# Two half-sized products of the down projection moved from the fourth-last block slot to the end, and the last product's two output tiles finished one by one

## What is computed

```python
def rmsnorm(x, g):
    xf = x.astype(jnp.float32)
    y = xf * lax.rsqrt(jnp.mean(xf * xf, axis=-1, keepdims=True) + EPS)
    return (y * g.astype(jnp.float32)).astype(x.dtype)

def swiglu(x, w_gate, w_up, w_down):
    return (jax.nn.silu(x @ w_gate) * (x @ w_up)) @ w_down
...
        xp = xp + swiglu(rmsnorm(xp, norm2_g[l]), w_gate[l], w_up[l], w_down[l])
...
    y_prompt = rmsnorm(xp, final_g)
```

## Time and profile before

| | |
|---|---|
| median of 3 executions | 2186.22 us (2185.85 to 2186.42) |
| the profiled execution | 2186.3 us |
| its span, first to last instruction | 2184.6 us |
| PE, matmuls: busy | 2170.5 us (99%) |
| VectorE: busy | 1714.3 us (78%) |
| ScalarE: busy | 1003.8 us (46%) |
| mean granted TensorE clock | 0.999 |
| moved by DMA | 325.63 MB, mean 149 GB/s |

### The profile page before, as it was taken

How to read it: one execution, slowest core, us unless ns; L and a number is a source line. 1 busy time by engine, 2 the same in 40 slices (tenths; PEclk the granted TensorE clock), 3 DMA queues, 4 the chain that set the end, 5 groups by cost and what they waited for, 6 DMA issues and landing times.

```text
span 2184.6 us, 40850 instructions
## 1 busy us (share of the span) xinstructions
PE 2170.5 (99%) x17316; PEld 2164.5 (99%) x17316; DVE 1714.3 (78%) x1988; ACT 1003.8 (46%) x1331; POOL 12.6 (1%) x16
## 2 busy tenths in 40 slices
PE   9999999999999999999999999999999999999997
PEld 9999999999999999999999999999999999999997
DVE  7765478446796789888887888888888888787888
ACT  7433523124354455444444544444444545444455
POOL 0000000000000000000000000000000000000001
PEclk9999999999999999999999999999999999999999
DMA  5332324245333434345445445444545876555523
GB/s 191 95 109 88 107 69 145 79 144 189 117 107 99 155 108 169 128 144 165 141 134 165 142 132 155 154 131 141 165 145 164 302 287 216 193 199 199 188 78 121
DMA packets 121584, 325.63 MB, mean 149 GB/s; under 512 B 10703, under 2 KB 51215, under 8 KB 120433
## 3 DMA queue, kind: packets, MB, share of 16 engines
q1 hardware_dynamic: 120928, 323.82, 44.1%
q10 hardware_dynamic: 528, 0.07, 0.0%
HBM read 267.22 MB, written 56.63 MB: 148 GB/s over the span
## 4 chain that ended last, share of the span: by engine, by line
PE 98%; DVE 1%; ACT 0%; issue 0%; POOL 0%; POOLq 0%; DVEq 0%; ACTq 0%
PE acc L1617 24%; PE acc L1302 21%; PE g L1617 18%; PE acc L1625 12%; PE g L1625 9%; PE acc L1526 2%; PE acc L1564 2%; PE g L1526 2%; PE g L1564 2%; PE g L1518 1%; PE acc L1518 1%; PE g L1329 0%; PE g L1452 0%; PE g L1321 0%; PE g L1459 0%; PE g L1351 0%
## 5 line engine op out<-in xcount | busy, mean ns | idle before, releaser
L1123 ACT CAST w_hi<-w_s 128x1024 fp32r<-128x1024 f32 (+1 forms) x204 | 209.1, 1025 | 356.0 <-DVE w_s L2414 349.8
L1617 PE MATMUL g<-op_hi,w_hi 128*128 128x272 f32 x1056 | 272.2, 288 | 0.0
L1617 PE MATMUL acc<-op_hi,w_hi 128*128 128x272 f32 x1056 | 271.6, 288 | 0.4 <-ACT acc L1097 0.4
L1617 PE MATMUL g<-op_lo,w_hi 128*128 128x272 f32 x1056 | 271.9, 288 | 0.0
L1617 PE MATMUL acc<-sg_hi,w_hi 128*128 128x272 f32 x1056 | 271.8, 288 | 0.0
L1617 PE MATMUL acc<-op_lo,w_hi 128*128 128x272 f32 x1056 | 271.4, 288 | 0.0
L1617 PE MATMUL acc<-sg_lo,w_hi 128*128 128x272 f32 x1056 | 271.4, 288 | 0.0
L1302 PE MATMUL acc<-op_hi,w_hi 128*128 128x272 f32 x1280 | 267.6, 290 | 0.0
L1302 PE MATMUL acc<-op_hi,w_lo 128*128 128x272 f32 x1280 | 264.8, 288 | 0.0
L1302 PE MATMUL acc<-op_lo,w_hi 128*128 128x272 f32 x1280 | 264.7, 288 | 0.0
L2389 DVE TENSOR_TENSOR w_lo<-w_s,w_hi 128x1024 fp32r<-128x1024 f32 (+1 forms) x204 | 242.7, 1190 | 11.8 <-ACT w_hi L1123 5.9
(11 more groups left out here) (390 smaller groups left out, 4672.7 us busy)
## 6 DMA issues: line engine op xcount, KB each, us to landing
w<-w_gu SPq DMA_DIRECT2D x88, 512.0 KB, 3.3
w_raw<-w_gu SPq DMA_DIRECT2D x88, 512.0 KB, 4.1
w_raw<-w_in SPq DMA_DIRECT2D x64, 512.0 KB, 3.6
hf_dram<-hf_hi SPq DMA_DIRECT2D x22, 952.0 KB, 6.5
hf_dram<-hf_lo SPq DMA_DIRECT2D x22, 952.0 KB, 8.8
w_raw<-w_d SPq DMA_DIRECT2D x32, 512.0 KB, 4.3
w<-w_d SPq DMA_DIRECT2D x26, 512.0 KB, 3.3
op_hi<-hf_dram SPq DMA_DIRECT2D x16, 544.0 KB, 7.1
```

The source lines that it names most:

```text
L1123: nc.scalar.copy(w_hi[:, (C_ST + n) % RING, 0:w], src[:, 0:w]).then_inc(hi_ready, 1)
L1617: nc.tensor.matmul(out, w_h, x, start=fresh and j == 0 and i == 0, stop=False, skip_group_check=True)
```

## The change

In slot 63 (`HELD`) only products 0, 1, 2, 5 and 4 run, in that order. Its products 3 and 6, which only concern the first half of the tokens, are computed at the end: the last slot runs nine, `0, 1, 2, 5, 4, 3, 3, 6, 6`, where the seventh and the ninth are slot 63's. For them SyncE loads blocks 3 and 2 of slot 63's weights again, into the two halves of `w_raw`, once the last slot's `sum_block` 2 has read these. The ring numbering shifts by two behind slot 63 (`at`).

Slot 63 then has no copy `pb` to `pd`: its C22 step adds `pb` to both token halves in one instruction of twice the width, once product 4 is done, and its C21 step is empty. C11 only needs product 0, and waits for `seeded`.

At the end, the row sums of the second half are computed between the two sides of the seventh product. The ninth product signals `side_done` after its first side; each of its two output tiles is added, squared, scaled with the gain and summed by PE on its own (`last_output`, `last_square`, `last_gain`). The squares of C11's part are added by VectorE instead of PE. The stores of the second half leave from other places of `y_second`, since product 3 still reads one that was used before.

```diff
+HELD = TAIL - 1
+HELD_ORDER = (0, 1, 2, 5, 4)
+LAST_ORDER = HELD_ORDER + (3, 3, 6, 6)
...
+            sp.wait_ge(s_made, 4 * NS - 1)
+            for i, j in enumerate((3, 2)):
+                sp.dma_start(w_raw[:, i, :], w_d4[4 * (HELD - FT - 2 * BATCHES) + j]).then_inc(held_in[i], 16)
...
             for s in range(1, NS - 1):
-                for idx in range(NP):
+                for idx in range(NP if s != HELD else len(HELD_ORDER)):
+                    if s == HELD and idx >= 3:
+                        bank_copy(s, idx + 1)
+                        block_hi(s, idx, copied=True)
+                        if idx == 4:
+                            bank_copy(s, 6)
+                        continue
...
             part_square(0)
+            act.wait_ge(chunk_done, done(at(NS - 1) + 3))
+            block_hi(NS - 1, 7, copied=True)
             part_square(1)
             act.wait_ge(c_read, 4 * NS + 4 + 2)
             seed_d(NS - 1)
+            act.wait_ge(chunk_done, done(at(NS - 1) + 4))
+            block_hi(NS - 1, 8, copied=True)
             part_gain(0)
             part_gain(1)
             row_std(1, pc[:, 1, 0:TH], 2)
             copy_factor(1, pc[:, 0, 0:TH], 1)
             part_square(2)
-            part_square(3)
             part_gain(2)
+            for q in range(2):
+                last_square(q)
+                last_gain(q)
             row_std(0, pa[:, 0, 0:TH], 3)
-            part_gain(3)
             copy_factor(0, pa[:, 1, 0:TH], 2)
...
+            product(C_ST + n + 6, n + 6, (0,), h, e_held, which=3, ends=False)
+            pe.wait_ge(c_read, read + 1)
+            pe.wait_ge(part_add, 1)
+            square_sums(pc[:, 1, 0:TH], (rstd[:, TH:T],))
+            product(C_ST + n + 6, n + 6, (1,), h, e_held, which=3)
+            down_wait(NS - 1, 6)
+            product(C_ST + n + 7, n + 7, (0, 1), h, e, which=6)
+            product(C_ST + n + 8, n + 8, (0,), h, e_held, which=6, ends=False).then_inc(side_done, 1)
+            product(C_ST + n + 8, n + 8, (1,), h, e_held, which=6)
             pe.wait_ge(c_read, read + 3)
-            pe.wait_ge(part_sq, 3)
-            square_sums(pa[:, 0, 0:TH], (rstd[:, 0:TH], sq4[2][:, 0, :], sq4[2][:, 1, :]), stop=False)
-            pe.wait_ge(part_sq, 4)
-            square_sums(pa[:, 0, 0:TH], (sq4[3][:, 0, :], sq4[3][:, 1, :]), start=False)
+            pe.wait_ge(part_add, 2)
+            square_sums(pa[:, 0, 0:TH], (rstd[:, 0:TH],), stop=False)
+            for q in range(2):
+                pe.wait_ge(part_sq, 4 + q)
+                square_sums(pa[:, 0, 0:TH], (sq4[3][:, q, :],), start=False, stop=q == 1)
...
-                dve.wait_ge(chunk_done, done(n + ((5, 4, 3, 6) if s == NS - 1 else (3, 4, 5, 6))[piece]))
+                dve.wait_ge(chunk_done, done(n + ((6, 4, 3, 8) if s == NS - 1 else (0, 4, 3, 4) if s == HELD else (3, 4, 5, 6))[piece]))
...
+                elif piece == C22 and s == HELD:
+                    nc.vector.tensor_tensor(y[:, :, 1, :, :], y[:, :, 1, :, :],
+                                            pb[:, :, 0:TH].unsqueeze(2).to_broadcast([P, 2, 2, TH]), ALU.add)\
+                        .then_inc(c_read, 1)
+                elif piece == C21 and s == HELD:
+                    dve.nop().then_inc(c_read, 1)
...
+            def last_output(q):
+                if q == 0:
+                    dve.wait_ge(side_done, 1)
+                else:
+                    dve.wait_ge(chunk_done, done(at(NS - 1) + 8))
+                y = rows(BATCHES - 1)[:, q, 1, 0, :]
+                nc.vector.tensor_tensor(y, y, pd[:, q, 0:TH], ALU.add).then_inc(c_read, 1)
+                dve.wait_ge(c_read, 4 * NS + 8 + q)
+                dve.nop().then_inc(y_part, 1)
...
             outputs(last, C22)
+            block_lo(last, 6)
             dve.wait_ge(hsq_add, 2 * KT - 2)
             add_part(0)
             add_part(1)
             dve.nop().then_inc(part_add, 1)
-            block_lo(last, 6)
+            block_lo(last, 7)
             row_factor(1, 1)
             outputs(last, C11)
             scale(1, pc[:, 0, 0:TH], (0,))
-            outputs(last, C21)
-            scale(1, pc[:, 0, 0:TH], (2, 4, 6))
+            block_lo(last, 8)
+            add_part(2)
+            dve.nop().then_inc(part_add, 1)
+            scale(1, pc[:, 0, 0:TH], (2,))
+            last_output(0)
+            scale(1, pc[:, 0, 0:TH], (4,))
+            last_output(1)
+            scale(1, pc[:, 0, 0:TH], (6, 8))
             row_factor(0, 2)
-            scale(1, pc[:, 0, 0:TH], (8,))
             scale(0, pa[:, 1, 0:TH], range(0, NV_OUT, 2))
```

More of the change, by code:

```diff
@@ L269, in build @@
         kv = trunk[:, 4:KT, :].rearrange("p (s m) t -> p s m t", s=NQ)
-        y_out = [[y[:, f, 0:HP, :] for f in range(4)] for y in (y_first, y_second)]
+        y_out = [[y[:, f, i:i + HP, :] for f, i in places]
+                 for y, places in ((y_first, ((0, 0), (1, 0), (2, 0), (3, 0))), (y_second, ((0, 0), (2, 0), (3, 0), (0, HP))))]
         aside = hid.rearrange("p (q r) t -> p q r t", q=2)
@@ L469, in product_at, with held_block @@
         def product_at(s, pos):
-            return LAST_ORDER[pos] if s == NS - 1 else pos
+            return LAST_ORDER[pos] if s == NS - 1 else HELD_ORDER[pos] if s == HELD else pos
+        def held_block(s, pos):
+            return s == NS - 1 and pos in (6, 8)
         def columns(s):
@@ L1087, in bank_copy @@
             def bank_copy(s, idx):
-                act.wait_ge(chunk_done, done(NP * s + idx - 4))
-                if idx == 1 and s >= 2:
+                act.wait_ge(chunk_done, done(at(s) + idx - 4))
+                if idx == 1 and s >= 2 and s - 1 != HELD:
                     seed_d(s - 1)
@@ L1114, in block_hi @@
                 which = product_at(s, idx)
-                if which in (0, 3):
+                src = block_of(s, which)
+                if held_block(s, idx):
+                    i = (6, 8).index(idx)
+                    act.wait_ge(held_in[i], 16)
+                    src = w_raw[:, i, :]
+                elif which in (0, 3):
                     act.wait_ge(blk_in[which], 16 * (s + 1))
@@ L1627, in product @@
                     last.then_inc(chunk_done, 1)
+                return last
             def quad(c, n, s, first=False, second=False):
@@ L1683, in _, with down_wait @@
                     quad(i * (4 * NP) + (C_ST + NP * q), NP * q, i * 4 + q)
+            def down_wait(s, idx):
+                if idx == 0:
+                    pe.wait_ge(c_read, 4 * s + C11 + 5)
+                elif idx == 1:
+                    pe.wait_ge(c_read, 4 * s + C12 + 5)
+                elif idx == 2:
+                    pe.wait_ge(seeded, s + 1)
+                elif idx == 4:
+                    pe.wait_ge(u2_out, s + 1)
+                elif idx == 5:
+                    pe.wait_ge(p5_out, s + 1)
+                elif idx == 6:
+                    pe.wait_ge(seeded_d, seeds_d(s))
             for s in range(FT, NS - 1):
                 ch, b = divmod(s - FT, BATCHES)
[L1686 to L1698, removed]
+                for pos, idx in enumerate(HELD_ORDER if s == HELD else range(NP)):
+                    down_wait(s, idx)
                     if b == 0:
                         pe.wait_ge(form_in[idx], 32 * (ch + 1))
-                    product(C_ST + NP * s + idx, NP * s + idx, (0, 1), PAIRS_H[ch], 4 * (ch % 2))
+                    product(C_ST + at(s) + pos, at(s) + pos, (0, 1), PAIRS_H[ch], 4 * (ch % 2), which=idx)
             def square_sums(out, bufs, start=True, stop=True):
@@ L1708, in square_sums @@
                     last.then_inc(var_done, 1)
[L1710 to L1728, removed]
@@ L1729, in _ @@
-            pe.wait_ge(c_read, read + 3)
-            pe.wait_ge(part_sq, 3)
-            square_sums(pa[:, 0, 0:TH], (rstd[:, 0:TH], sq4[2][:, 0, :], sq4[2][:, 1, :]), stop=False)
-            pe.wait_ge(part_sq, 4)
-            square_sums(pa[:, 0, 0:TH], (sq4[3][:, 0, :], sq4[3][:, 1, :]), start=False)
+            n, read = at(NS - 1), 4 * NS + 4
+            h, e, e_held = PAIRS_H[NCH - 1], 4 * ((NCH - 1) % 2), 4 * ((NCH - 2) % 2)
+            for pos, idx in enumerate(HELD_ORDER + (3,)):
+                down_wait(NS - 1, idx)
+                product(C_ST + n + pos, n + pos, (0, 1), h, e, which=idx)
@@ L2629, in _ @@
                         sum_block(s, 2)
+                    if s == HELD and idx == 2:
+                        sum_block(s, 3)
                     if idx == 2 and FT < s <= TAIL:
                         summands(s - 1)
-                    if idx == 3:
+                    if idx == 3 and s != HELD:
                         sum_block(s, 3)
```

42 lines of the change are left out of this document (28 added, 14 removed).

## The result

The changed kernel takes **2189.32 us** (median of 20, 2189.07 to 2190.16) against 2186.02 us before (median of 20): a ratio of 1.0015, 95% interval 1.0008 to 1.0022. That is 3.3 us more, inside the 0.2% that I had named as the bound of "no change", and just inside the range (2184.2 to 2189.4), but 2.5 us above the forecast of 2186.8.

A forecast was written before the change was run, and what follows sets the result against it. The prediction took PE's matmul stream and what follows it as the bound. Stall +2.86, tail -1.76 and stores -0.5 summed to +0.6 us, giving 2186.8 us, with an 8-in-10 range of 2184.2 to 2189.4.

The forecast's parts named there:

- The frame and slot 63: Around slot 63: 3.00 us a product, 21.02 a slot, PE's total unchanged, no wait there or for slot 64's loads.
- The stall in slot 64: Slot 64: C22 of slot 63 waits for product 4, delaying VectorE's queue and the seeded copy; PE stalls 2.86 us.
- The tail: End of the last slot: second root at 2171.38 against 2173.14 in the frame before, a win of 1.76 us.
- Rival 3: Last slot: VectorE late, low part 8's 0.4 us cover gone or side adds behind scales, +0.5 to 2 us; chance 0.13.
- Rival 4: Tail isn't shortened because the DMA engines bind anyway: +2.9 us, 2189.1; chance 0.05.
- Rival 1: Slot 64: PE isn't held for the copy, only the tail's win is left: 2183.9 us; chance 0.12.
- The stores: Behind the second root: the first half's first store finds DMA engines free, winning 0 to 0.7 us, taken as 0.5.
- Rival 2: Slot 64: PE's holes drop the granted clock; one product at 1.2 GHz gives 2189.8, two 2192.8 us; chance 0.05.

The follow-up runs named there:

- the run with the copy first: Changed kernel with ScalarE's copy pa to pb in slot 64 placed ahead of the casts of products 2 and 3: 2189.03 us.
- GpSimd later alone: Changed kernel with GpSimd starting to scale the second half's tiles only after VectorE has added the squares of C11's part: 2186.91 us.
- the run with both repairs: Changed kernel with C22 of slot 63 added after product 1's low part in slot 64, and GpSimd's scaling held until C11's squares are added: 2184.02 us.
- the run of the second part alone: Kernel before with the last product's tiles finished singly and C11's squares added by VectorE, no product held back: 2190.33 us.

## Why the prediction was right, and where it failed

- **The frame and slot 63: right.** PE's busy time didn't change, slot 63 has no late side, and the held loads and slot 64's loads are in no wait.
- **The stall in slot 64: right**, 3.03 us against 2.86, and by the step named (C22 can't start before the end of product 4). Moving that one add takes 2.96 us off. What the prediction didn't say is whose time it is: VectorE's, as the run with the copy first showed.
- **The tail: wrong, and this is the step that failed.** The prediction has "low part 8 from 2171.7 to 2172.9", then two adds, each at the usual length. The start was right, the lengths weren't. These lengths came from rows in which GpSimd was idle. In the kernel before no VectorE instruction with two SBUF inputs ran while GpSimd scaled: the scales and C11's add read one input from PSUM. The change puts three such instructions behind GpSimd's start, and GpSimd later alone gives 2.41 us back. In the changed kernel two of them ran beside it, low part 8 and the first add. PE then waited 0.73 us inside the ninth product, for low part 8, where the prediction had 0.4 us of cover. With the cause removed (the run with both repairs) the tail wins 1.54 up to the root, where 1.76 was worked out.
  The rule was there to be read. The Trainium skill ("SBUF — State Buffer", section "Who interferes with whom") says that a VectorE instruction with two SBUF inputs contends with a GpSimd one that reads SBUF, and one with at most one SBUF input, outside VectorE's two-port modes, doesn't. The runs agree on both halves: 2.42 against 1.23 us for low part 8, and 0.72 as ever for a scale.
- **Rival 3** (VectorE late in the last slot, 2187.3 to 2188.8, chance 0.13) is the case that came, for a reason it didn't name, and 0.5 us above its upper end.
- **Rival 4** (no shorter tail since the DMA engines bind, 2189.1, chance 0.05) has nearly the measured time, but not its mechanism: the loss lies ahead of the root, and behind it 0.52 was won. **Rival 1** (no stall in slot 64) is out.
- **The stores: right**, 0.52 against 0.5. And by the step named: when the first half's first store was issued (2180.34), the DMA engines had been idle since 2180.00 (share 0.00). In the kernel before they were still at work in the 0.66 us ahead of that store (share 0.67).
- **Rival 2: right to be small**, but its argument doesn't carry. With holes of 0.3 to 1.6 us the clock stayed at 1.00. The prediction took from one row that the clock holds for several microseconds of nothing; in the run of the second part alone it held for about 2.
- **The range: luck.** It held the time by 0.1 us only. It was worked out from a tail whose uncertainty was put at 2 us; the miss in the tail was 2.59 (0.83 + 1.76), with the wrong sign.

## What to carry to other kernels

When a step is moved, ask not only what it waits for, but what runs beside it in its new place: a duration read where GpSimd was idle doesn't hold beside GpSimd if the instruction reads two tensors from SBUF. When an instruction with a late input stands in the list of an engine that is nearly full, letting PE's other inputs come sooner may only move the wait (0.7 of 1.0 us came back here); move the late instruction behind the work that is ready. And a change that comes out near zero can hold a gain and two losses of its own size: each was worth 2 to 3 us here, and one step moved took each loss away.

## What the runs showed of the hardware

- VectorE and GpSimd exclude each other by whole instructions when both read two tensors from SBUF. A 272-column add, 0.44 us alone, took 1.45 to 1.64 us beside GpSimd instructions of about 1.35 us, and 0.90 to 1.02 beside ones of 0.77. The other side waits too: GpSimd's three scalings took 5.00 us instead of 3.94. A scale with one of its two inputs in PSUM took 0.72 beside GpSimd, as alone.
- With PE idle for 4.0 us in the run of the second part alone, the granted clock averaged 0.82 over 2170 to 2172 and was 0.50 from 2172 on, and stayed there until the end, through the last sums. It fell about 2.0 us behind PE's last matmul; in the kernel before it fell about 5.0 us behind it.
